# Gate projections cut by depth instead of by token half, in a hybrid attention and Mamba-2 layer

## The chip, the cores and the metric

The kernel runs on one core of a Trainium2 chip, as one launch. The metric is the device time in microseconds (us) of the whole launch. The engines named below are TensorE (PE, matmuls into PSUM), ScalarE (ACT), VectorE (DVE), GpSimd (POOL, here only a DMA queue) and SyncE (SP, a DMA queue). They run their own instruction streams in order and meet only at semaphores.

## The reference

One trunk layer over 128 context and 512 latent tokens, width 1024. What matters here is the mixer: one input projection gives attention heads, the scan's inputs, `z` and the gates, and the gates are used much later.

```python
def mixer(h, p, rope, ctx_k, ctx_v, h0_f, h0_b):
    proj = h @ p['w_in']
    q, k, v, z, xbc, dt, gates = jnp.split(proj, SPLIT_IDX, axis=-1)
    ...
    y_f, h_f = ssd_chunked(xs, dt_f, a[0], bm, cm, h0_f)
    y_b, h_b = ssd_chunked(flip(xs), flip(dt_b), a[1], flip(bm), flip(cm), h0_b)
    ...
    y = rms_norm(y * jax.nn.silu(z), p['ssd_norm'])
    g_a, g_b = jnp.split(gates, 2, axis=-1)
    merged = jax.nn.sigmoid(g_a) * (attn @ p['w_attn_o']) + jax.nn.sigmoid(g_b) * (y @ p['w_ssd_o'])
    return merged @ p['w_out'], k, v, h_f, h_b
```

## The kernel before

**Arithmetic.** Every large product is made of three matmuls of rounded parts, upper by upper (`whi`, `hh`), upper by lower (`whi`, `hl`) and lower by upper (`wlo`, `hh`). A block of weights is 1024 by 256. It comes by DMA into `raw` (`block` in the SP stream, L390), ACT rounds it into `whi` (`split_hi`, L1284) and DVE writes the rest into `wlo` (`split_lo`, L1749). There are two slots. Slot s is rounded anew only when PE has used it up, so `split_hi` of a block stands in ACT's stream right behind the read of the last result of the block two before.

**The scan with filling.** From about 523 to 906 us the kernel runs the Mamba-2 scan, chunk by chunk. Its steps are short and hang on each other across PE, ACT and DVE, so PE gets large independent matmuls between them, called pieces, written out by hand in a fixed order. `fill(n)` issues the next n pieces on PE, `weights(n)` does what belongs to the same pieces on ACT and on DVE, `weights(n)` in the SP stream issues weight loads (through `block_done`), and `stores(n)` on POOL writes results out. The first 40 pieces are tiles of `z`. The other 32 (n = 0 to 31) are the gate projections: 16 units of 128 gate channels, each over all 644 token columns, which lie in two halves of 322 columns (`HALF`) in two PSUM banks, `acc[:, 0]` and `acc[:, 1]`. Before the change a piece is one half: piece 2u fills bank 0 over the whole depth of 1024 (8 steps `k`, 24 matmuls), piece 2u + 1 fills bank 1. A piece waits until the piece two before it, which used the same bank, has been read out (`value(free, 2)`). ACT reads each piece out as soon as it comes to it (`out_of_acc`, L1296, 322 columns), and POOL stores a unit after its second piece.

**Where the pieces stand.** The scan has four latent chunks c = 1 to 4. Each runs `fill(F_LAT[c - 1])`, that is 3 pieces in a row, then `products`, then eight groups g = 0 to 7 with `fill(F_LAT_G[g])` and `scan_group(g, b, c)`; `F_LAT_G` is 1, 0, 1, 0, 1, 1, 0, 1. With the z tiles counted off, the gate pieces stand so:

- chunk 1: n = 0, 1, 2, 3 at groups 2, 4, 5, 7
- chunk 2: n = 4, 5, 6 at the start, then 7, 8, 9, 10, 11 at groups 0, 2, 4, 5, 7
- chunk 3: n = 12, 13, 14, then 15 to 19 likewise; chunk 4: n = 20, 21, 22, then 23 to 27
- behind the scan (`F_END` = 4): n = 28 to 31, and then attention

**What ACT has between the pieces at a chunk's start.** `exps(n)` (L1510, L1515) makes the decay weights of a group, and `squares(c, q)` (L1526) sums the squares of a gated quarter of y, which DVE has to have written (`gated`, L2050):

```python
            for c in range(1, NT):
                weights(1)
                exps(NG * c)
                if c > 1:
                    squares(c - 1, 2, zq[:, 0])
                weights(1)
                exps(NG * c + 1)
                if c > 1:
                    squares(c - 1, 3, zq[:, 1])
                weights(F_LAT[c - 1] - 2)
```

In front of the last quarters DVE has, in the group 7 of the chunk before: the lower part of a weight block (`split_lo`), `carried` (L2017 to L2031), `combined` (L2037) and `gated`.

**The z loads.** `z_in(c, q)` in the SP stream (L526) fetches a quarter of z for `gated(c, q)`; it stands behind group `Z_STEPS[q]` and waits for an earlier `squares`. In group 7 the SP stream also has a weight block (L390, 1 MB), which waits for a `split_lo`, and `h_in(c + 1, 1)` (L466, 512 KB).

The functions that the change touches, with the line numbers of the profile:

Of the kernel before, what the change touches and what calls it, by code (L numbers as in the profile page):

```python
# [8 lines left out]
ACT = mybir.ActivationFunctionType  # L9
# [4 lines left out]
P = 128  # L14
D = 1024
KT = D // P
# [22 lines left out]
HALF = TP // 2  # L39
NCONV = CTX + 2 + LAT  # L40
BW = 256
# [20 lines left out]
def value(c, back=0):  # L62

    v = c["step"] * (c["base"] + c["k"] - back)
    assert v > 0, "a wait stands where there is something to wait for"
    return v if c["round"] is None else c["round"] * (c["per"] * c["step"]) + v


def step(c, n=1):

    c["k"] += n
    return c["step"]


def due(c, back=0):

    step(c)
    return value(c, back)
# [27 lines left out]
def build(nc, a, outs):  # L106
# [16 lines left out]
    with ExitStack() as ctx:  # L123
# [207 lines left out]
        U_QKV = U_XBC + 2 * XBC // BW  # L331
        U_Z = U_QKV + 6 * NT
        U_G = U_Z + DI // BW * NT
        U_AO = U_G + 4 * 2 * D // BW
        U_SO = U_AO + KT
        U_OUT = U_SO + KT
        U_H2 = U_OUT + 4 * NT
# [18 lines left out]

        Y_ORDER = (1, 2, 3, 4, 0)
        Y_OUT = (1, 1, 2, 2, 3)
        Z_STEPS = (1, 2, 4, 6)
        GATED = {8 + 2 * q: q for q in range(4)}  # L360

        def block_done(p):
# [310 lines left out]
        def _(po):  # L673
# [65 lines left out]
            def stores(n):  # L739
                for p in range(pieces["k"], pieces["k"] + n):  # L740
                    if p < N_ZP:
                        step(free)
                        b, t = p // NT, p % NT
                        if t in (2, NT - 1):
                            part, z = (slice(0, 3), zo[0]) if t == 2 else (slice(3, NT), zo[1])
                            po.wait_ge(free["sem"], value(free))
                            po.dma_start(z_d.rearrange("t p c -> p t c")[:, part, b * BW:(b + 1) * BW],
                                         zst[:, part]).then_inc(z["sem"], step(z))
                    elif (p - N_ZP) % 2 == 1:
                        u = (p - N_ZP) // 2  # L750
                        step(free, 2)
                        po.wait_ge(free["sem"], value(free))
                        po.dma_start(g_d[u], gst[:, u % 2]).then_inc(go[u % 2]["sem"], step(go[u % 2]))
                step(pieces, n)

# [43 lines left out]
        def _(pe):  # L799
# [5 lines left out]
            def mul(out, l, r, first=True, last=True):  # L805
                return pe.matmul(out, l, r, start=first, stop=last)  # L806
# [203 lines left out]
                                   k == 0 and w is whi and m is hh, k == KT - 1 and m is hl)  # L1010
                last.then_inc(ready["sem"], step(ready))

            def gate_piece(n):

                unit, half = n // 2, n % 2
                slot, sub = unit // 2 % 2, unit % 2
                if n % 4 == 0:
                    pe.wait_ge(lo["sem"], due(lo))
                step(free)
                pe.wait_ge(free["sem"], value(free, 2))  # L1020
                for k in range(KT):
                    for w, m in ((whi, hh), (whi, hl), (wlo, hh)):
                        last = mul(acc[:, half, 0:HALF], w[:, slot, k, sub * P:(sub + 1) * P],
                                   m[:, k, half * HALF:(half + 1) * HALF],
                                   k == 0 and w is whi and m is hh, k == KT - 1 and w is wlo)
                last.then_inc(ready["sem"], step(ready))

            def fill(n):
                for p in range(pieces["k"], pieces["k"] + n):
                    if p < N_ZP:  # L1030
                        z_tile(p)
                    else:
                        gate_piece(p - N_ZP)
                step(pieces, n)

            btin, ctin, bnin = count(s["bt_in"], 16), pair("ct_in"), pair("bn_in")
# [238 lines left out]
        def _(act):  # L1275
# [17 lines left out]
            def out_of_acc(dst, src, func):  # L1293

                act.wait_ge(ready["sem"], due(ready))
                act.activation(dst, src, func).then_inc(free["sem"], step(free))  # L1296
# [175 lines left out]
            def weights(n):  # L1472

                for p in range(pieces["k"], pieces["k"] + n):
                    b = block_done(p)
                    if p < N_ZP:
                        z = zo[p % NT // 3]
                        if p % NT in (0, 3):
                            step(z)
                            act.wait_ge(z["sem"], value(z, 1))  # L1480
                        act.wait_ge(ready["sem"], due(ready))
                        act.activation(zst[:, p % NT], acc[:, p % 2, 0:BW], ACT.Tanh, scale=0.5).then_inc(s["zt_ok"], 1)
                    else:
                        u, half = (p - N_ZP) // 2, p % 2
                        if half == 0:
                            if u == 0:
                                for z in zo:
                                    act.wait_ge(z["sem"], value(z))
                            step(go[u % 2])
                            act.wait_ge(go[u % 2]["sem"], value(go[u % 2], 1))  # L1490
                        out_of_acc(gst[:, u % 2, half * HALF:(half + 1) * HALF], acc[:, half, 0:HALF], ACT.Copy)
                    if b is not None:
                        split_hi(b % 2)
                step(pieces, n)
# [866 lines left out]
```

## Time and profile before

| | |
|---|---|
| time before, median of 3 runs | 1839.19 us (1834.86 to 1839.99) |
| the profiled execution's own time | 1839.19 us |
| its span, first to last instruction | 1837.5 us |
| PE busy with matmuls | 1632.3 us (89% of the span) |
| DVE busy | 1031.7 us (56%) |
| ACT busy | 663.7 us (36%) |
| mean granted TensorE clock | 0.937 of full speed |

Times inside the profile count from the span's start. An engine's row in the timeline has its start, its duration, the line and the operation, what it writes and reads, how many instructions are merged, and in brackets how long the engine sat idle before it and who released it. Matmuls overlap: one of 322 columns is shown as 0.31 us, and the next starts 0.15 us behind it. A matmul is preceded by a weight load (LDWEIGHTS, the PEld rows). A row of a window has its bounds and length, then the busy time in it of PE, PEld, DVE, ACT and POOL with the number of instructions, then the granted clock of TensorE as a share of full speed (2.4 GHz; the other level is 1.2), the DMA engines' busy share and GB/s.

### The profile page before, as it was taken

How to read it: one execution, taken by the hardware profiler on the slowest of the kernel's cores; microseconds unless marked ns; L12 is line 12 of the kernel's file. 1: busy time of each engine (PE TensorE's matmuls, PEld its weight loads, DVE VectorE, ACT ScalarE, POOL GpSimd, SP SyncE). 2: the span in 40 equal slices, each digit the busy share in tenths (PEclk: the TensorE clock that was granted, in tenths of full speed). 3: DMA queues.
4: the chain of work that ended last, by engine and by line, in shares of the span. 5: the costliest groups of instructions: out<-in, count | busy, mean ns of one | idle time of the engine just before them, and what ended most of it. 6: DMA issues, size and time to landing. Idle time of an engine off the chain costs nothing.

```text
span 1837.5 us, 27440 instructions
## 1 busy us (share of the span) xinstructions
PE 1632.3 (89%) x11141; PEld 1538.5 (84%) x11141; DVE 1031.7 (56%) x1419; ACT 663.7 (36%) x1115; POOL 99.3 (5%) x155
## 2 busy tenths in 40 slices
PE   4799999989998998989799899989299999999995
PEld 2699988889998988888655699989199999999995
DVE  5466666556845578887555353335843343342467
ACT  4544443334365246667355432311321121111210
POOL 1000012110011100000000001000000000000000
PEclk9799999899999999999899999999599999999998
DMA  9344345532486676676600255342011222223221
GB/s 309 99 134 136 124 142 187 174 116 75 138 264 206 221 241 213 200 240 189 236 23 23 71 184 179 112 174 70 23 44 56 84 68 68 68 68 91 69 68 57
DMA packets 159721, 241.14 MB, mean 131 GB/s; under 512 B 8048, under 2 KB 126560, under 8 KB 156576
## 3 DMA queue, kind: packets, MB, share of 16 engines
q1 hardware_dynamic: 136464, 171.45, 28.8%
q0 software_dynamic: 12304, 47.72, 7.0%
q10 hardware_dynamic: 10880, 20.97, 4.2%
q8 instruction: 49, 0.80, 0.2%
q14 instruction: 24, 0.20, 0.0%
HBM read 195.06 MB, written 45.06 MB: 131 GB/s over the span
## 4 chain that ended last, share of the span: by engine, by line
PE 74%; DVE 14%; ACT 7%; issue 2%; DMA 1%; SPq 0%; ACTq 0%; DVEq 0%
PE acc L806 66%; PE tp L806 6%; DVE arena L1849 2%; ACT arena L1510 1%; DVE wlo L1749 1%; PE tp L1188 1%; DVE arena L2002 1%; ACT whi L1284 1%; DMA arena<-in_w_mod 1%; DVE arena L1788 1%; DVE arena L1787 1%; PE tp L889 1%; DVE wlo L1800 1%; DVE arena L2004 1%; DMA y_nat<-arena 1%
## 5 line engine op out<-in xcount | busy, mean ns | idle before, releaser
L806 PE MATMUL acc<-hh,whi 128*128 128x322 f32 x1408 | 363.4, 325 | 16.6 <-DVE wlo L1749 7.2
L806 PE MATMUL acc<-hl,whi 128*128 128x322 f32 x1408 | 357.4, 321 | 0.0
L806 PE MATMUL acc<-hh,wlo 128*128 128x322 f32 x1408 | 354.9, 319 | 0.0
L806 PEld LDWEIGHTS acc<-hh,whi 128*128 128x128 f32 x1408 | 254.1, 198 | 18.7 <-issue 12.2
L806 PEld LDWEIGHTS acc<-hl,whi 128*128 128x128 f32 x1408 | 255.2, 198 | 0.0
L806 PEld LDWEIGHTS acc<-hh,wlo 128*128 128x128 f32 x1408 | 254.1, 197 | 0.0
L1284 ACT ACTIVATE whi<-raw 128x2048 fp32r<-128x2048 f32 x78 | 148.7, 1908 | 266.2 <-PE acc L806 266.2
L1749 DVE TENSOR_TENSOR wlo<-raw,whi 128x2048 fp32r<-128x2048 f32 x78 | 178.5, 2290 | 101.5 <-ACT whi L1284 101.2
L806 PE MATMUL acc<-whi,hh 128*128 128x256 f32 x720 | 206.9, 287 | 8.0 <-DVE hl L2237 8.0
L806 PE MATMUL acc<-whi,hl 128*128 128x256 f32 x720 | 203.6, 283 | 0.0
L806 PE MATMUL acc<-wlo,hh 128*128 128x256 f32 x720 | 203.6, 283 | 0.0
L806 PE MATMUL acc<-whi,fh 128*128 128x256 f32 x640 | 183.2, 286 | 15.2 <-DVE fl L2299 15.2
L806 PE MATMUL acc<-wlo,fh 128*128 128x256 f32 x640 | 183.3, 286 | 0.0
L806 PE MATMUL acc<-whi,fl 128*128 128x256 f32 x640 | 182.8, 286 | 0.0
L806 PEld LDWEIGHTS acc<-whi,hh 128*128 128x128 f32 x720 | 137.4, 191 | 8.8 <-issue 8.4
L806 PEld LDWEIGHTS acc<-whi,fh 128*128 128x128 f32 x640 | 124.5, 195 | 16.3 <-issue 16.3
L806 PEld LDWEIGHTS acc<-wlo,hh 128*128 128x128 f32 x720 | 137.0, 190 | 0.3
L806 PEld LDWEIGHTS acc<-whi,hl 128*128 128x128 f32 x720 | 137.0, 190 | 0.0
L806 PE MATMUL tp<-arena 128*128 128x64 f32 (+3 forms) x508 | 115.6, 373 | 15.0 <-DVE arena L2004 10.0
L806 PEld LDWEIGHTS acc<-wlo,fh 128*128 128x128 f32 x640 | 124.3, 194 | 0.0
L806 PEld LDWEIGHTS acc<-whi,fl 128*128 128x128 f32 x640 | 124.2, 194 | 0.0
L1849 DVE SCALAR_TENSOR_TENSOR arena<-arena,colp 128x642 f32<-128x642 f32 x128 | 113.7, 888 | 18.7 <-DVE arena L1847 1.2
(255 smaller groups left out, 2327.0 us busy)
## 6 DMA issues: line engine op xcount, KB each, us to landing
raw<-in_w_in SPq DMA_DIRECT2D x38, 1024.0 KB, 7.0
raw<-in_w_mlp SPq DMA_DIRECT2D x32, 1024.0 KB, 5.4
arena<-in_w_mod SPq DMA_DIRECT2D x24, 1024.0 KB, 6.3
arena<-decay_sums_t ACTq DMA_DIRECT2D x40, 512.0 KB, 5.5
arena<-xs_nat SPq DMA_DIRECT2D x8, 1024.0 KB, 8.0
raw<-in_w_ssd_o SPq DMA_DIRECT2D x8, 1024.0 KB, 6.0
y_nat<-arena POOLq DMA_DIRECT2D x6, 1024.0 KB, 7.2
arena<-y_nat SPq DMA_DIRECT2D x6, 1024.0 KB, 6.4
```

The lines of the kernel that those rows point to most:

```text
L806: return pe.matmul(out, l, r, start=first, stop=last)
L889: last = pe.transpose(dst, cvs[:, n % 2, tok(t):tok(t) + P], ident)
L1188: last = pe.transpose(tp[:, j // 4, (j % 4) * P:(j % 4 + 1) * P], pr[:, u, j * P:(j + 1) * P], ident)
L1284: act.activation(whi[:, slot], raw[:, slot], ACT.Copy).then_inc(hi["sem"], step(hi))
L1510: last = act.activation(ee[:, b, d, r], abc[:, b, d, r], ACT.Relu, bias=dta[:, c, h:h + 1], scale=-1.0)
L1749: dve.tensor_tensor(wlo[:, slot], raw[:, slot], whi[:, slot].bitcast(F32), ALU.subtract).then_inc(lo["sem"], step(lo))
L1787: do(dve.scalar_tensor_tensor(x, x, mv[:, t, 0:1], rows[:, 0], ALU.subtract, ALU.mult))
L1788: return dve.scalar_tensor_tensor(x, x, mv[:, t, 2:3], rows[:, 1], ALU.mult, ALU.add)
L1800: dve.tensor_tensor(dst, src, upper.bitcast(F32), ALU.subtract).then_inc(mlo["sem"], step(mlo))
L1849: ins = dve.scalar_tensor_tensor(o, x[:, t:t + NCONV], w(t), o, ALU.mult, ALU.add)
L2002: last = dve.tensor_tensor(ee[:, b, d], ee[:, b, d], cbm[:, d, g].unsqueeze(1).broadcast_to([P, R, P]), ALU.mult)
L2004: dve.tensor_tensor(ee[:, b, 0], ee[:, b, 0], ee[:, b, 1], ALU.add).then_inc(m_ok["sem"], step(m_ok))
```

## The change

Three things change.

- A gate piece becomes half of the depth instead of half of the tokens (`gate_half`). Piece 2u runs k = 0 to 3 into both banks, piece 2u + 1 runs k = 4 to 7 into both banks. The matmuls of the two halves of the tokens with the same weights now stand next to each other. The number of matmuls in a piece stays 24, and their shape is the same.
- A unit is finished only with its second piece. Only then is it signalled, ACT reads both banks with one instruction of 644 columns, and `acc_ready` and `acc_free` count units and not pieces (`U_AO`). The first piece of a unit waits until the unit before has been read (`value(free, 1)`).
- `Z_STEPS` goes from (1, 2, 4, 6) to (1, 2, 5, 7).

```diff
@@ -331,7 +331,7 @@
         U_QKV = U_XBC + 2 * XBC // BW
         U_Z = U_QKV + 6 * NT
         U_G = U_Z + DI // BW * NT
-        U_AO = U_G + 4 * 2 * D // BW
+        U_AO = U_G + 2 * 2 * D // BW
         U_SO = U_AO + KT
         U_OUT = U_SO + KT
         U_H2 = U_OUT + 4 * NT
@@ -356,7 +356,7 @@
 
         Y_ORDER = (1, 2, 3, 4, 0)
         Y_OUT = (1, 1, 2, 2, 3)
-        Z_STEPS = (1, 2, 4, 6)
+        Z_STEPS = (1, 2, 5, 7)
         GATED = {8 + 2 * q: q for q in range(4)}
 
         def block_done(p):
@@ -748,8 +748,7 @@
                                          zst[:, part]).then_inc(z["sem"], step(z))
                     elif (p - N_ZP) % 2 == 1:
                         u = (p - N_ZP) // 2
-                        step(free, 2)
-                        po.wait_ge(free["sem"], value(free))
+                        po.wait_ge(free["sem"], due(free))
                         po.dma_start(g_d[u], gst[:, u % 2]).then_inc(go[u % 2]["sem"], step(go[u % 2]))
                 step(pieces, n)
 
@@ -1010,27 +1009,30 @@
                                    k == 0 and w is whi and m is hh, k == KT - 1 and m is hl)
                 last.then_inc(ready["sem"], step(ready))
 
-            def gate_piece(n):
-
-                unit, half = n // 2, n % 2
+            def gate_half(n):
+
+                unit, part = n // 2, n % 2
                 slot, sub = unit // 2 % 2, unit % 2
                 if n % 4 == 0:
                     pe.wait_ge(lo["sem"], due(lo))
-                step(free)
-                pe.wait_ge(free["sem"], value(free, 2))
-                for k in range(KT):
+                if part == 0:
+                    step(free)
+                    pe.wait_ge(free["sem"], value(free, 1))
+                for k in range(4 * part, 4 * part + 4):
                     for w, m in ((whi, hh), (whi, hl), (wlo, hh)):
-                        last = mul(acc[:, half, 0:HALF], w[:, slot, k, sub * P:(sub + 1) * P],
-                                   m[:, k, half * HALF:(half + 1) * HALF],
-                                   k == 0 and w is whi and m is hh, k == KT - 1 and w is wlo)
-                last.then_inc(ready["sem"], step(ready))
+                        for half in range(2):
+                            last = mul(acc[:, half, 0:HALF], w[:, slot, k, sub * P:(sub + 1) * P],
+                                       m[:, k, half * HALF:(half + 1) * HALF],
+                                       k == 0 and w is whi and m is hh, k == KT - 1 and w is wlo)
+                if part == 1:
+                    last.then_inc(ready["sem"], step(ready))
 
             def fill(n):
                 for p in range(pieces["k"], pieces["k"] + n):
                     if p < N_ZP:
                         z_tile(p)
                     else:
-                        gate_piece(p - N_ZP)
+                        gate_half(p - N_ZP)
                 step(pieces, n)
 
             btin, ctin, bnin = count(s["bt_in"], 16), pair("ct_in"), pair("bn_in")
@@ -1480,15 +1482,14 @@
                             act.wait_ge(z["sem"], value(z, 1))
                         act.wait_ge(ready["sem"], due(ready))
                         act.activation(zst[:, p % NT], acc[:, p % 2, 0:BW], ACT.Tanh, scale=0.5).then_inc(s["zt_ok"], 1)
-                    else:
-                        u, half = (p - N_ZP) // 2, p % 2
-                        if half == 0:
-                            if u == 0:
-                                for z in zo:
-                                    act.wait_ge(z["sem"], value(z))
-                            step(go[u % 2])
-                            act.wait_ge(go[u % 2]["sem"], value(go[u % 2], 1))
-                        out_of_acc(gst[:, u % 2, half * HALF:(half + 1) * HALF], acc[:, half, 0:HALF], ACT.Copy)
+                    elif (p - N_ZP) % 2 == 1:
+                        u = (p - N_ZP) // 2
+                        if u == 0:
+                            for z in zo:
+                                act.wait_ge(z["sem"], value(z))
+                        step(go[u % 2])
+                        act.wait_ge(go[u % 2]["sem"], value(go[u % 2], 1))
+                        out_of_acc(gst[:, u % 2].rearrange("p (a b) -> p a b", a=2), acc[:, 0:2, 0:HALF], ACT.Copy)
                     if b is not None:
                         split_hi(b % 2)
                 step(pieces, n)
```

## Rows read from the trace of the kernel before

**Rows 1.** Windows over chunks 3 and 4.

```profile
769.39:827.24 57.85, 51.44 (x322) 49.25 (x322) 48.19 (x68) 37.57 (x91) 2.69 (x5) 0.94 0.72 232
827.24:885.57 58.33, 50.71 (x306) 49.05 (x306) 42.38 (x58) 37.45 (x91) 2.69 (x5) 0.88 0.52 158
```

**Rows 2.** The chain that ended last, chunk 3: start us, us, what.

```profile
769.58 10.79 PE acc L806 x72
...
782.16 3.58 PE acc L806 x24
785.76 0.44 ACT arena L1296
...
788.03 2.29 DVE wlo L1749
...
792.31 7.39 PE acc L806 x32
```

**Rows 3.** Timeline of PE, chunk 2: the first matmul of piece 6.

```profile
718.93 0.31 PE L806 MATMUL acc<-hh,whi 128*128 128x322 f32 x1
```

**Rows 4.** Timeline of ACT, start of chunk 2.

```profile
721.72 0.63 ACT L1526 ACTIVATE cst<-arena 128x512 f32<-128x512 f32 x1 [1.73 <-DVE arena L2050]
...
722.35 0.42 ACT L1296 ACTIVATE arena<-acc 128x322 f32<-128x322 f32 x1
```

**Rows 5.** Groups by form on ACT: the two sizes of read-out of L1296.

```profile
L1296 ACT ACTIVATE arena<-acc 128x644 f32<-128x644 f32 x32 | 22.7, 710 | 99.4 <-PE acc L806 99.4
...
L1296 ACT ACTIVATE arena<-acc 128x322 f32<-128x322 f32 x32 | 13.6, 430 | 44.6 <-PE acc L806 44.6
```

**Rows 6.** Chain, PE's waits (total us, times, longest), PE's timeline, a window.

```profile
879.39 5.55 PE acc L806 x24
...
896.81 8.90 PE acc L806 x48
...
PE acc L806 <- ACT arena L1296: 4.4, 2, 3.8
...
734.64 0.69 PE L806 MATMUL acc<-arena 128*128 128x64 f32 x2 [3.16 <-DVE arena L2004]
...
731.40:742.00 10.60, 7.44 (x35) 7.34 (x35) 10.39 (x16) 7.25 (x19) 0.00 (x0) 0.68 1.00 358
```

**Rows 7.** Timelines of PE (chunks 3 and 4) and of ACT (chunk 4).

```profile
821.86 1.10 PE L806 MATMUL tp<-arena 128*128 128x64 f32 x8 [1.79 <-DVE arena L2004]
...
867.64 0.40 PE L806 MATMUL acc<-hh,whi 128*128 128x322 f32 x1
...
877.42 1.97 PE L806 MATMUL tp<-arena 128*128 128x64 f32 x8 [3.32 <-DVE arena L2004]
...
868.46 0.42 ACT L1296 ACTIVATE arena<-acc 128x322 f32<-128x322 f32 x1
```

**Rows 8.** Timeline of PE, a later stage that already pairs its matmuls.

```profile
1046.77 0.46 PE L806 MATMUL acc<-hl,whi 128*128 128x322 f32 x2
1047.07 0.46 PE L806 MATMUL acc<-hh,wlo 128*128 128x322 f32 x2
```

**Rows 9.** DVE at the start of chunk 3 and behind chunk 4.

```profile
780.00 0.69 DVE L2050 TENSOR_TENSOR arena<-arena,cst 128x512 f32<-128x512 f32 x1
...
782.20 1.23 DVE L1994 TENSOR_TENSOR arena<-tp,cst 128x1024 f32<-128x1024 f32 x1 [0.90 <-PE tp L806]
...
894.98 0.69 DVE L2050 TENSOR_TENSOR arena<-arena,cst 128x512 f32<-128x512 f32 x1
```

**Rows 10.** SP issues; then DMA issues with size and median us to landing.

```profile
773.92 0.46 SPq L466 DMA_DIRECT2D arena<-h_back  x1
...
889.55 0.38 SPq L390 DMA_DIRECT2D raw<-in_w_attn_o  x1
...
arena<-h_back SPq DMA_DIRECT2D x1, 512.0 KB, 6.2
...
cst<-z_nat SPq DMA_DIRECT2D x2, 256.0 KB, 11.3
```

## The prediction

> **What bounds the kernel now.** I read the page first, then the windows by chunk, then the chain that ended last inside the scan, and last the timelines of PE, ACT and DVE around every piece that the change touches.
>
> The page has PE busy 89% of the span. That says little about the changed stretch, because the matmuls of this stretch are the filling of a chain of short steps. The windows show it: a chunk lasts 57.85 us, and the next 58.33 us, with DVE busy 48.19 and 42.38 us of them [rows 1]. No engine is full, so the order of the waits decides.
>
> The chain of chunk 3 shows which waits those are [rows 2]. It begins on PE: three pieces in a row (10.79 us for 72 matmuls), `products`, and piece 15 (3.58 us). Then ACT reads piece 15 out (0.44 us), rounds a weight block (until 788.03), DVE writes its lower part (2.29, to 790.32) and weights group 1. Only then PE goes on at 792.31. The reader is to see two things. The first 16 us of each chunk run on PE alone, so whatever delays PE there delays the chunk. And nothing runs beside the chain that could take a delay in: piece 15 is what ACT and DVE wait for.
>
> **Part 1, the order of the matmuls.** The count stays 24 per piece, 768 in all, each with its own weight load. Before, neighbours have different weights, and 72 take 10.79 us, which is 150 ns each and 3.60 us for a piece [rows 2]. A later stage that already has neighbours with the same weights takes 0.30 us for two, from 1046.77 to 1047.07 [rows 8], the same 150 ns. I cost this part at 0.
>
> The Trainium skill, "TensorE: Matmul & The Clock Gate", section "Step-by-step: what each phase is for", says that weights typically stay put over many matmuls, so that one load can serve several. The trace does not show that here, since the paired stage runs at the same pace; what the rule would give stands with the rivals.
>
> **Part 2, the wait of a unit's first piece.** It is now behind the read-out of the whole unit before. There are 15 such places. ACT's place in its stream matters more than the length of its read-out.
>
> *Pieces 6, 14 and 22*, the third of three in a row. Before the change, piece 6 needed only piece 4's read-out, which ACT did in front of `exps`. Now it needs that of pieces 4 and 5, and this stands in ACT's stream behind `exps` and behind `squares(c - 1, 2)`, which waits for DVE. The rows give the moment: the `squares` start at 721.72, when DVE has let them go, and the read-out of piece 5 follows at 722.35 [rows 4]. Piece 6 began at 718.93 [rows 3]. After the change:
>
> - the read-out at 722.35 comes 0.28 us later, because what DVE waited for began with the read-out of piece 3, now 710 ns and not 430 [rows 5]: 722.63
> - it takes 0.71 us itself [rows 5]: 723.34, and some 0.05 us to PE: 723.4
>
> So piece 6 starts 4.45 us late. Chunks 3 and 4 repeat this pattern at the same offsets, so it is 3 x 4.45 = 13.4 us. By [rows 2] all of it is on the chain. What was queued behind piece 6 on PE is `products`, piece 7, and with it the weight block, group 1 and the rest. DVE's own wait in front of `products` (0.90 us [rows 9]) only grows.
>
> *The clock behind these waits.* PE sits idle some 4.3 us there. Before, it already goes idle once in each chunk, ahead of group 1: 3.16 us in chunk 2, and the window around that has a granted clock of 0.68 [rows 6], so most of it ran at 1.2 and not at 2.4 GHz. What this costs is read from the chain: behind the same idling in chunk 3, 8 scan matmuls and a piece take 7.39 us [rows 2], where full clock gives 1.10 [rows 7] + 3.60 = 4.70 us, so 2.7 us; behind 877.42 it is 1.97 + 5.55 - 4.70 = 2.8 us [rows 6, 7]; behind the 3.8 us of idling ahead of 896.81, 48 matmuls take 8.90 us and not 7.2, so 1.7 us [rows 6]. The bounds are 0 and 2.8. I take 2.3: 3 x 2.3 = 6.9 us.
>
> *Pieces 2, 10, 18 and 26* at group 5. They now wait for the unit that ended at group 4, which ACT reads behind an `exps`. In chunk 4 this read-out starts at 868.46 and would end at 869.17, where piece 26 began at 867.64 [rows 7]: 1.6 us late. But PE idles 3.32 us soon after, ahead of 877.42 [rows 7], so this costs nothing, and it cuts that idling into about 1.4 and 1.7 us. Idling of that length (1.79 us ahead of 821.86) left the clock up: the 8 matmuls behind it took 1.10 us, not 1.97 [rows 7]. I therefore expect the slow stretch behind 877.42 to go: -2.8 us. The bound on the other side is 0. In the other three chunks the wait is 0.5 us, in front of an idling of 1.3 us; nothing.
>
> *Pieces 4, 8, 12, 16, 20, 24 and 28* stand behind a scan group or behind a read-out that is long done: 0.1 us at most. *Piece 30* is in part 4.
>
> **Part 3, one read-out of 644 columns.** It is 0.28 us longer than one of 322 [rows 5]. On the chain it stands behind pieces 7, 15 and 23, ahead of the rounding of a block: 3 x 0.28 = 0.8 us. That of pieces 3, 11 and 19 is in part 2 already. ACT loses 16 of 32 read-outs, about 16 x 0.43 x 2 - 16 x 0.71 = 2.4 us of work, none of it on the chain.
>
> **Part 4, the z loads and the end.** Moving the third from behind group 4 to behind group 5 changes nothing, since the SP stream has nothing between. The fourth is moved past the weight block and past `h_in`, and these wait for a `split_lo` of group 7. It is issued at about 774.4 instead of before 764. `h_in`, issued at 773.92 behind the block, landed after 6.2 us, at 780.1 [rows 10], so this quarter of z should land at about 781. `gated` wanted it at 780.00, and DVE then waited until 782.20 for `products` [rows 9], which now come 4 us later still. So 0, three times; without that cover it would be 1 us each.
>
> Behind chunk 4 there is no cover. The load is issued right behind the block of 889.55 [rows 10], so at about 890.2 with the longer read-out before it, and lands near 896, where `gated` started at 894.98 [rows 9]: 0.8 us. The worst landing of such loads in the trace is 11.3 us [rows 10], which would make it 6. The chain to piece 30 also has the longer read-outs of pieces 27 and 29, and behind 31 a third: 0.8 us. For a somewhat longer slow clock behind piece 30 I add 0.5. Together 2.1 us.
>
> **The sum.** 13.4 + 6.9 - 2.8 + 0.8 + 2.1 = 20.4 us on the profiled execution's 1839.19 us, which is also the median: 1859.6 us, rounded to 1860. Behind the scan nothing changes, and attention starts from piece 31's read-out, so the delay should arrive whole.
>
> **The rivals.**
>
> *A. Only the read-out itself is waited for* (no measurable change). The wait of pieces 6, 14, 22 and 30 would be the 0.71 us of the read-out and a signal, so 0.75 x 4 = 3 us, and no slow clock. With the read-outs on the chain (0.8 + 0.8) and no saved slow stretch: 1844 us; with it 1841. It needs ACT to be free when piece 5 ends. For it: ACT has an idle stretch of 1.73 us there. Against it: that idling ends with `squares`, which stand ahead of the read-out [rows 4].
> The Trainium skill, "Perfetto Trace Analysis", section "Matmuls", has the rule behind it, that independent groups should rotate through PSUM banks so that the read-out of one runs beside the next. It speaks against this change, and by it alone the price is one read-out per unit in a row; the trace agrees that before, with two banks in turn, piece 6 had no wait.
>
> *B. Matmuls with the same weights run faster* (faster than before). The weight loads fill PE's load side as much as the matmuls do (49.25 us of loads beside 51.44 us of matmuls in chunk 3 [rows 1]), so if the loads set the 150 ns and half of them became free, a matmul would go down. 28 of the 32 pieces lie on the chain (not those at group 5), 672 matmuls. It outweighs the 20.4 us from 30 ns each, and shows as faster from (20.4 + 5.5) / 672 = 39 ns; at a pace of 110 ns the time would be 1859.6 - 26.9 = 1833 us. Against it stands the equal pace of the stage that pairs them [rows 8].
> The sentence of the Trainium skill on loading once, cited above, would lead here; by it the change is a gain, and the paired stage does not bear it out.
>
> *C. The z loads are late as well* (slower still). If the fourth quarter lands 11.3 us after its issue [rows 10], that is at 785.7, DVE is still done before `products` come at about 786.8, so only the end pays: 5 us more, 1865; with a clock price of 2.8 and no saved stretch behind 877.42, 1869 us.
>
> **How the numbers follow.** The forecast, three waits of more than 4 us with a slow clock behind them, has 0.78; C has 0.08, A 0.08, B 0.06. What a measurement of this kernel can tell from no change is 0.3%, 5.5 us. The forecast's own range: with clock prices of 0 to 2.8 us, the saved stretch there or not, and the end at 1.6 to 7 us, it runs from 1839.2 + 13.4 + 0 - 2.8 + 0.8 + 1.6 = 1852 to 1839.2 + 13.4 + 8.4 + 0.8 + 7 = 1869. To 1850 and 1868 leaves out A and B and a little of C, under 2 in 10. A is half below 1845, so slower by over 0.3% is 0.87, within it 0.08, faster 0.05.
>
> **What would show it.** In the profile after, PE should sit idle about 4.3 us ahead of the third piece of chunks 2, 3 and 4, put down to ACT L1296, and the piece behind it should take about 5.5 us and not 3.6. The three chunk windows should grow by about 7 us each, chunk 4's by less, with granted clocks under 0.94. L1296 should have 16 read-outs fewer of 322 and 16 more of 644 columns at 710 ns. The matmuls inside a piece should keep 150 ns. It would be wrong if ACT reads pieces 4 and 5 before `squares`, if the idle stretch is there but the clock stays up, or if DVE's `gated` waits for a DMA ahead of `products`.

## The result and the profile after

| | before | after |
|---|---|---|
| median | 1838.51 us (1834.86 to 1839.99, 4 runs) | 1858.80 us (1855.09 to 1859.84, 4 runs) |
| the profiled execution: time, span | 1839.19, 1837.5 us | 1860.62, 1858.9 us |
| mean granted clock | 0.937 | 0.936 |

The ratio is 1.011, 95% interval [1.0089, 1.0131]: slower by 1.1%, and 1.2 us from the forecast of 1860. The read-out is L1298 now, the matmul L805, `squares` L1527, `gated` L2051.

First the windows, from one chunk start to the next (chunks 2, 3, 4):

```profile
709.67:773.91 64.24, 53.59 (x321) 50.89 (x321) 48.20 (x68) 37.23 (x87) 2.72 (x5) 0.92 0.66 209
773.91:840.05 66.14, 55.45 (x321) 52.75 (x321) 48.20 (x68) 37.22 (x87) 2.70 (x5) 0.90 0.64 203
840.05:903.50 63.45, 51.82 (x304) 49.65 (x305) 42.47 (x58) 37.11 (x87) 2.70 (x5) 0.87 0.45 146
```

Chunks 3 and 4 took 57.85 and 58.33 us [rows 1], chunk 2 took 57.69 (its pieces 4 and 12 start at 711.70 and 769.39). The three sum to 193.83 us instead of 173.87, so 20.0 us come in here. DVE is busy as long as before (48.20 us in chunk 3, before 48.19), ACT a little less (37.2 and 37.6). PE's clock is lower, 0.92, 0.90 and 0.87 against 0.94 and 0.88 in [rows 1].

The chain that ended last shows what the length is. The rows start at the beginning of chunk 3, with the `gated` of the third quarter of the y of chunk 2 (start us, us, what; in all chains "..." stands for rows left out):

```profile
783.23 0.70 DVE arena L2051
...
784.49 0.19 ACT cst L1527
784.67 0.60 ACT arena L1298
...
785.32 5.35 PE acc L805 x24
790.67 1.78 PE tp L805 x16
792.46 3.61 PE acc L805 x24
```

In chunk 3 before, the chain began on PE and stayed there for 16 us [rows 2]. Now it comes out of DVE: `gated`, then ACT's `squares` (the row at 784.49 is their end), then the read-out of pieces 12 and 13, and only then the third piece, 14. PE's timeline puts the idle time at that same point, and ACT's timeline in chunk 2 shows the order on its side:

```profile
785.32 0.68 PE L805 MATMUL acc<-hh,whi 128*128 128x322 f32 x2 [4.06 <-ACT arena L1298]
```

```profile
719.72 0.63 ACT L1527 ACTIVATE cst<-arena 128x512 f32<-128x512 f32 x1 [4.37 <-DVE arena L2051]
...
720.35 0.69 ACT L1298 ACTIVATE arena<-acc 128x644 f32<-128x644 f32 x1
```

ACT sits idle for 4.37 us in front of `squares`. The read-out that PE waits for stands behind them in ACT's stream, and its second piece was done at 717.07. The three idle stretches of PE are 4.02, 4.06 and 4.06 us. The third pieces behind them take 5.21, 5.35 and 6.44 us, where the piece in the chain above, at 792.46, takes 3.61. In the groups by form the read-outs of 322 columns are gone:

```profile
L1298 ACT ACTIVATE arena<-acc 128x644 f32<-128x644 f32 x48 | 33.9, 706 | 145.3 <-PE acc L805 145.3
```

That is 16 more than the 32 of [rows 5]. The end of the scan, on the same chain:

```profile
896.30 1.10 PE tp L805 x8
897.41 5.16 PE acc L805 x24
...
905.20 2.30 DVE wlo L1750
...
907.52 0.38 SPq L390
...
907.95 6.36 DMA cst<-z_nat
...
914.40 0.70 DVE arena L2051
...
915.85 0.60 ACT arena L1298
...
916.50 9.94 PE acc L805 x48
```

The last quarter of z is on the chain: it is asked for only when the lower part of the weight block is written and the next block issued (907.52). From piece 28 to the end of piece 31 it is 22.9 us (903.50 to 926.4), where it was 20.1 (885.57 to 905.7). The first four matmuls of attention then take 2.93 us instead of 1.56. DVE's waits for z, in total, times, longest:

```profile
DVE arena L2051 <- DMA cst<-z_nat: 13.5, 4, 4.6
```

Before there was no such wait. Three of the four are off the chain. DVE's timeline in chunk 3 shows why:

```profile
789.15 0.69 DVE L2051 TENSOR_TENSOR arena<-arena,cst 128x512 f32<-128x512 f32 x1 [4.63 <-DMA cst<-z_nat]
...
792.50 1.23 DVE L1995 TENSOR_TENSOR arena<-tp,cst 128x1024 f32<-128x1024 f32 x1 [2.05 <-PE tp L805]
```

DVE loses 4.63 us to the fourth quarter of z, and then still has to wait 2.05 us for `products`, which are late themselves.

From the start of piece 28 to the end of the span, before took 951.9 us and after 955.4: +3.5. With the +20.0 this is 23.5 us; the two spans differ by 21.4, because chunk 2 began 2.0 us earlier in this execution (709.67 against 711.70). That start scatters from run to run: in the kernels below that add nothing to PE's program it lies between 702.31 and 713.33.

### The profile page after: what moved, and what is told of

Read it like the earlier page. It is cut to its first block, busy times and chain, and to the rows that moved or that the text cites. A ratio compares the mean times of both kernels' runs of the same rounds, so it can differ in the third digit from the quotient of the medians.

```text
span 1858.9 us, 27421 instructions
## 1 busy us (share of the span) xinstructions
PE 1638.2 (88%) x11141; PEld 1542.0 (83%) x11141; DVE 1031.8 (56%) x1419; ACT 662.4 (36%) x1099; POOL 99.5 (5%) x155
## 4 chain that ended last, share of the span: by engine, by line
PE 72%; DVE 15%; ACT 7%; issue 3%; DMA 2%; SPq 0%; ACTq 0%; DVEq 0%
PE acc L805 64%; PE tp L805 5%; DVE arena L1850 2%; DVE wlo L1750 2%; ACT arena L1511 1%; ACT whi L1286 1%; PE tp L1190 1%; DVE arena L2003 1%; DMA arena<-in_w_mod 1%; PE tp L888 1%; DVE arena L1789 1%; DVE arena L1788 1%; ACT arena L1298 1%; DVE wlo L1801 1%; DVE arena L2005 1%
## 5 line engine op out<-in xcount | busy, mean ns | idle before, releaser
L805 PE MATMUL acc<-hh,whi 128*128 128x322 f32 x1408 | 343.3, 326 | 33.3 <-ACT arena L1298 20.1
L805 PE MATMUL acc<-hl,whi 128*128 128x322 f32 x1408 | 336.5, 321 | 0.0
L805 PE MATMUL acc<-hh,wlo 128*128 128x322 f32 x1408 | 333.2, 319 | 0.0
L805 PEld LDWEIGHTS acc<-hh,whi 128*128 128x128 f32 x1408 | 248.0, 199 | 37.1 <-ACT arena L1298 21.7
L805 PEld LDWEIGHTS acc<-hl,whi 128*128 128x128 f32 x1408 | 250.5, 198 | 0.0
L805 PEld LDWEIGHTS acc<-hh,wlo 128*128 128x128 f32 x1408 | 248.8, 197 | 0.0
L805 PE MATMUL acc<-whi,hh 128*128 128x256 f32 x720 | 207.6, 288 | 7.9 <-DVE hl L2238 7.9
L805 PE MATMUL acc<-whi,hl 128*128 128x256 f32 x720 | 204.3, 284 | 0.0
L805 PE MATMUL acc<-wlo,hh 128*128 128x256 f32 x720 | 204.1, 283 | 0.0
L805 PE MATMUL acc<-whi,fh 128*128 128x256 f32 x640 | 182.7, 285 | 15.2 <-DVE fl L2300 15.2
L805 PE MATMUL acc<-wlo,fh 128*128 128x256 f32 x640 | 182.7, 286 | 0.0
L805 PE MATMUL acc<-whi,fl 128*128 128x256 f32 x640 | 182.4, 285 | 0.0
L805 PEld LDWEIGHTS acc<-whi,hh 128*128 128x128 f32 x720 | 138.1, 192 | 8.8 <-issue 8.4
L805 PEld LDWEIGHTS acc<-wlo,hh 128*128 128x128 f32 x720 | 137.7, 191 | 0.3
L805 PEld LDWEIGHTS acc<-whi,hl 128*128 128x128 f32 x720 | 137.6, 191 | 0.0
L805 PEld LDWEIGHTS acc<-whi,fh 128*128 128x128 f32 x640 | 124.0, 194 | 16.3 <-issue 16.3
L805 PE MATMUL tp<-arena 128*128 128x64 f32 (+3 forms) x508 | 113.9, 370 | 11.9 <-DVE arena L2005 8.4
L805 PEld LDWEIGHTS acc<-wlo,fh 128*128 128x128 f32 x640 | 123.8, 193 | 0.0
L805 PEld LDWEIGHTS acc<-whi,fl 128*128 128x128 f32 x640 | 123.6, 193 | 0.0
```

## The experiments

"Sum of the chunks" below is always the three windows of chunks 2, 3 and 4: 173.87 us before, 193.83 us in the profile after. "Behind piece 28" is from its start to the end of the span: 951.9 us before, 955.4 after. "Waits" are PE's idle times ahead of pieces 6, 14 and 22, and these are the "third pieces". All of these are of one profiled execution; the ratio is that of the times to the kernel before, measured beside it on the same chip.

### The changed kernel again

The changed kernel as it is, measured once more.

> The changed kernel as it is, beside the others of this call, for a ratio with as many runs as theirs. 1.0110 of the kernel before, as first measured, within 0.2%.

1.0129 [1.0108, 1.0151]; waits 4.05, 4.06, 4.02; third pieces 6.50, 5.23, 5.35; sum of the chunks 190.56, behind piece 28 955.0. The sum is 3.3 us less than in the first profile of the same kernel. Two slow stretches, 8 scan matmuls and piece 19 or 27, ran at full clock this time (pieces 19 and 27 take 3.84 us, and took 5.06 and 5.34). The timelines of PE ahead of piece 19, first of the profile after, then of this run:

```profile
832.81 1.47 PE L805 MATMUL tp<-arena 128*128 128x64 f32 x8 [1.79 <-DVE arena L2005]
```

```profile
835.96 1.10 PE L805 MATMUL tp<-arena 128*128 128x64 f32 x8 [1.78 <-DVE arena L2005]
```

The same idle time before, at one and the same place, once with the clock low and once not.

### The waits without the pairs

```diff
-                for k in range(4 * part, 4 * part + 4):
+                half = part
+                for k in range(KT):
                     for w, m in ((whi, hh), (whi, hl), (wlo, hh)):
-                        for half in range(2):
...
```

The order of the matmuls of before, with all waits, read-outs and z loads of the changed kernel.

> The changed kernel with its waits, its one read-out of 644 columns per unit and its Z_STEPS, but the matmuls in the old order: the first piece of a unit fills one bank over the whole depth, the second the other, so no neighbours share weights. My theory (the order of the matmuls costs and gives nothing): the same time as the changed kernel, 1857 to 1861. Rival B in the weak form that pairing gives some ns per matmul back: 1863 to 1870.

1.0126 [1.0111, 1.0141], against 1.011 and 1.0129 with pairs. Waits 4.03, 4.03, 4.01; third pieces 6.47, 5.18, 5.38; sum of the chunks 190.57, where the changed kernel has 190.56. The pairs are worth nothing. Rival B falls.

### Read out before the squares

```diff
                 weights(1)
                 exps(NG * c)
+                weights(1)
                 if c > 1:
                     squares(c - 1, 2, zq[:, 0])
-                weights(1)
                 exps(NG * c + 1)
```

> The changed kernel with one move in ACT's stream: at the start of chunks 2 to 4 the read-out of the first unit stands ahead of squares(c - 1, 2) and not behind it. My theory: PE's wait ahead of pieces 6, 14 and 22 falls from 4.0 us to about 0.7 (the read-out of 0.71 us and a signal) and the clock stays up there, so 3 x (3.3 + 1.6 to 2.8) = 15 to 18 us come back: 1841 to 1845. If not the place in ACT's stream but something else of the changed structure costs the time: 1855 to 1859.

1.0028 [1.0014, 1.0042], so 0.01 lower than the changed kernel as measured again, some 18 us (15 against its first ratio). ACT's timeline in chunk 2, then PE's:

```profile
720.83 0.71 ACT L1298 ACTIVATE arena<-acc 128x644 f32<-128x644 f32 x1 [1.81 <-PE acc L805]
723.38 0.64 ACT L1527 ACTIVATE cst<-arena 128x512 f32<-128x512 f32 x1 [1.84 <-DVE arena L2051]
```

```profile
721.59 0.56 PE L805 MATMUL acc<-hh,whi 128*128 128x322 f32 x2 [0.86 <-ACT arena L1298]
```

ACT now waits for PE, reads at once, and PE stands still for 0.86 us and not 4.05. The third pieces take 3.83 us, so the low clock behind them is gone too. The sum of the chunks is 178.07. This is rival A's time (one read-out and a signal), made by moving one line. What made the wait dear was ACT's order and not the read-out.

### The z loads alone, and all but them

In the one kernel only `Z_STEPS` of before becomes (1, 2, 5, 7); in the other only `Z_STEPS` of the changed kernel goes back to (1, 2, 4, 6).

> The kernel before with the new Z_STEPS alone. My theory (the time comes from three waits of PE for ACT's read-out, which stands behind squares, and from the slow clock behind them): the late fourth quarter of z costs little. At the chunk boundaries DVE waits about 1 to 2 us for it, but products come 4 us sooner here than in the changed kernel, so up to 1 us per boundary may reach the chain; at the end of the scan 1 to 3 us. Time 1840 to 1844. Rival C (the z loads are what costs): 1850 or more. No effect at all: 1838.5.

> The changed kernel with the old Z_STEPS. My theory: PE's waits of 4.0 us ahead of the third piece of chunks 2, 3 and 4 stay; the end of the scan gets back about 2 us of the 5.6 us of idling ahead of piece 30. Time 1855 to 1858 against 1858.8. Rival C: under 1850.

Alone: 1.0018 [1.0007, 1.003]. Taken back: 1.0096 [1.0076, 1.0117]. DVE's waits, then PE's timeline ahead of piece 30, both of the kernel with the z loads alone:

```profile
DVE arena L2050 <- DMA cst<-z_nat: 4.9, 4, 1.3
```

```profile
899.27 0.64 PE L806 MATMUL acc<-hh,whi 128*128 128x322 f32 x1 [5.12 <-ACT arena L1296]
```

The sum of the chunks is 173.56, as before, although three of the waits lie there: they are covered. Behind piece 28 it is 955.2, +3.3: 1.3 us more idle (5.12 against 3.84), the 48 matmuls behind it 10.06 us and not 8.90, and attention's first four 2.93 and not 1.56, all three seen in the trace; 0.5 us of it is made up later. With the z steps taken back, the changed kernel's idle time is 4.14 us and `gated` waits for no DMA; behind piece 28 it is 952.5, so 2.5 us less than the changed kernel. The two ratios, 1.0129 and 1.0096, differ by 6 us, but their intervals leave room for anything from next to nothing to twice that.

### Both repairs

The changed kernel with `weights(1)` ahead of the squares and the old z steps.

> The changed kernel with both repairs: the first unit of chunks 2 to 4 is read out ahead of squares, and the old Z_STEPS. What is left of the change is the paired order, one read-out per unit and waits of under 1.5 us. My theory: within 0.2% of the kernel before (ratio 0.999 to 1.002), since read_before_squares gave 1.0028 and the z loads alone 1.0018. A rival by which the pairs pay would show as under 0.998.

1.0029 [1.0012, 1.0046]: a miss. Waits 0.86 three times, behind piece 28 952.7, but the sum of the chunks 180.39, 6.5 us above before, where three waits of 0.86 explain 2.6. In chunks 2 and 3 the piece at group 7 is slow (766.70 to 771.98 and 828.34 to 833.55, so 5.3 and 5.2 us, where it takes 3.8 in before). Much of what was left looked like clock, so the next kernels keep PE from falling idle.

### Matmuls in the wait

24 matmuls of 190 columns into unused PSUM columns, behind the second piece of three in a row (n = 5, 13, 21). Their result is used nowhere.

```diff
+                if n in (5, 13, 21):
+                    last = keep_busy(24)
                 if part == 1:
                     last.then_inc(ready["sem"], step(ready))
```

> The changed kernel with 24 extra matmuls of 190 columns, whose results nobody reads, behind pieces 5, 13 and 21; they fill part of the idle 4.0 us and carry the signal that the unit is done. They split the price of a wait from the price of the clock behind it. My theory: the third pieces still start when they did, but take 3.6 to 3.8 us and not 5.2 to 6.4, so 3 x 1.6 to 2.8 = 5 to 8 us come back: ratio to the kernel before 1.0065 to 1.0085. If the slow clock is not set off by this idling: no change, 1.011. If the extra matmuls last longer than the wait: slower.

1.0133 [1.011, 1.0156], no gain: a miss. Yet in the chunks it did what it was to do: idle 1.40, 1.35, 1.41 us, third pieces 3.83, 3.82, 3.84. The sum is 186.86 and not 190.56, so 3.7 us come back and not 5 to 8; pieces 19 and 27 were slow again here (5.23 and 5.35 us). Behind piece 28 it took 962.0 us, 7 more than the changed kernel, in stages that the edit does not touch. PE's waits behind 1300 us (in total, times, longest) have a row that the changed kernel doesn't have there:

```profile
PE acc L805 <- issue: 3.3, 2, 1.7
```

"issue" is idle time in which PE waited for nothing that the profile shows. These waits are 3.3 of the 7 us; the rest is not placed.

### The kernel before, kept busy at group 1

20 such matmuls ahead of group 1 of each latent chunk, behind a wait for the read-out of the piece before.

> The kernel before with 20 extra matmuls of 190 columns, whose results nobody reads, in the idling ahead of group 1 of chunks 1 to 4 (3.2 to 4.0 us), where the clock falls. If the slow clock follows from the idling: each of the four stretches behind it (7.0 to 7.45 us) falls to about 4.7, so 9 to 11 us less, ratio 0.994 to 0.995. If the extra matmuls outlast DVE's work: the gain is smaller or gone. If the clock falls for another reason: 1.000.

1.0023 [1.0006, 1.0039]: a miss, for two reasons. The stretches behind group 1 do run at full clock (4.73 us in chunk 4 and not 7.45), but three times 2.5 to 2.7 us give only 3.9 in the chunks (58.05, 57.57, 54.33). Piece 11 was slow in this execution (5.12 us, before 3.81), which takes 1.3 of the rest. The chain that ended last shows more, in chunk 2 and then in chunk 3:

```profile
728.52 1.21 DVE arena L2010 x2
...
730.37 0.68 DVE arena L1997
731.05 0.60 DVE arena L2025
731.65 0.61 DVE arena L2027
```

```profile
779.05 12.32 DMA arena<-decay_sums_t
...
793.88 9.22 DMA arena<-decay_sums_t
```

From 728.52 to 758.66 it runs on DVE with hardly a gap. In chunk 3 it runs over two loads of the decay sums that `exps` needs; the chain of the kernel before has none there. So with PE faster, DVE in one chunk and these loads in another are the next bound. And behind piece 28 it is 956.9 us, +5.0, again with "issue" waits (3.2 us in 2).

### Only a longer program

288 waits on a count long reached, ahead of the first turning of x. They come to 144 more wait instructions on PE (the trace has 144 instructions more). No work is added.

```diff
+            for _ in range(288):
+                pe.wait_ge(s["rows_in"], 16 * 9)
             turn_x(xin, "xn_ok", NT)
```

> The kernel before with 144 wait instructions more in TensorE's program (288 waits in the source, two to an instruction), ahead of the first turning of x, each on a count that is long reached; no other work is added or moved. Two kernels with dummy matmuls (24 behind pieces 5, 13 and 21 of the changed kernel; 20 ahead of group 1 in the kernel before) both took some 5 us longer in the MLP stage, which holds none of the dummies, with TensorE's idle put down to 'issue' there (3.2 to 3.3 us). Theory (A): the length of TensorE's program ahead of the MLP's loop sets where its instructions lie, and the fetch of them stalls; then this kernel is some 5 us above before, ratio 1.0020 to 1.0035, with the same 'issue' waits in the MLP stage. Rival (B): the dummies cost the MLP their time through the clock or through order of the work, not through the program's length; then this kernel is within 1.5 us of before (ratio 0.999 to 1.001), and shows no such 'issue' waits.

1.008 [1.0061, 1.0099], more than expected. PE's timeline where they stand, then PE's waits behind 1300 us:

```profile
68.46 1.94 PE L847 MATMUL acc<-cst,arena 128*128 128x128 f32 x8 [11.73 <-issue]
```

```profile
PE acc L806 <- issue: 5.5, 3, 1.9
```

PE stands for 11.7 us at the 144 instructions, some 81 ns each, which I had left out; chunk 2 starts only 6.2 us later (717.88), so a part is made up on the way. Behind piece 28 it is 960.3 us, +8.4, of which 5.5 are the "issue" waits; behind two of the three the clock is low as well. So rival B falls, and of theory A this much holds: a longer program of PE, with no matmul added, brings the waits in the MLP. That it is the fetch of instructions is not shown. Nor is length alone the rule: the last three kernels have 126 added matmuls, some 256 instructions with their weight loads, and none of them shows an "issue" wait there. So these three can be compared with the kernels that have no such wait.

### The changed kernel kept busy, 126 matmuls

24 behind n = 5, 13, 21 and 29, and 15 ahead of group 1 of chunks 2 and 3.

> The changed kernel with 24 dummy matmuls of 190 columns behind pieces 5, 13, 21 and 29, and 15 ahead of group 1 in chunks 2 and 3, so that TensorE doesn't stand idle through the 4 us waits; 126 matmuls, some 256 instructions more in all. Theory (A), the clock's fall costs what its stretches show (third pieces 6.4, 5.2, 5.3 against 3.83, sum about 5.5 us; some of it given back by the vector engines): chunk periods sum to 183 to 187 us against 190.6 of the changed kernel, and the time lies 3 to 7 us below it, ratio to before 1.009 to 1.011, if the MLP stage is as long as in the changed kernel; with the MLP's 5 us on top, ratio 1.012 to 1.014. Rival (B), what the low clock costs is only exchanged for waits for VectorE: the sum stays within 2 us of 190.6, ratio 1.012 to 1.014 with no MLP stall.

1.0069 [1.005, 1.0088]. PE's timeline in chunk 2, and the three windows:

```profile
720.55 2.82 PE L805 MATMUL acc<-hh 128*128 128x190 f32 x24
724.72 0.57 PE L805 MATMUL acc<-hh,whi 128*128 128x322 f32 x2 [1.36 <-ACT arena L1308]
```

```profile
713.31:774.98 61.67, 55.16 (x360) 52.66 (x360) 48.10 (x68) 37.23 (x87) 2.71 (x5) 0.97 0.66 218
774.98:836.60 61.62, 55.14 (x360) 52.64 (x360) 48.11 (x68) 37.24 (x87) 2.69 (x5) 0.97 0.66 218
836.60:897.10 60.50, 51.53 (x328) 49.45 (x329) 42.46 (x58) 37.22 (x87) 2.69 (x5) 0.94 0.46 152
```

The waits are as long as before (2.82 + 1.36 us), but filled. The clock is 0.97, 0.97 and 0.94, the sum 183.79, 6.8 us under 190.56, inside theory A's 183 to 187; rival B falls. Behind piece 28 it is 951.6, 3.4 less than the changed kernel, as the 48 matmuls of pieces 30 and 31 now take 7.4 us and not 9.6. A had left this gain out, so the ratio came out below its range of 1.009 to 1.011.

### The kernel before, and the repaired one, kept busy with as many

22 matmuls behind piece 29 and 104 at groups 1 (in the kernel before 84 there and 20 at group 6 of chunk 4).

> The kernel before with 22 dummy matmuls of 190 columns behind piece 29, 21 ahead of group 1 of chunks 1 to 4, and 20 ahead of group 6 of chunk 4: 126 matmuls, some 256 instructions more. The dummies fill the idle after which the clock was seen to fall. Theory (A), VectorE is the chain once the stretches run at full clock: the latent stage is 0 to 3 us shorter, and with no stall in the MLP the time is 0.998 to 1.000 of before, with it 1.000 to 1.003. Rival (B), the low clock is paid in full: four stretches of 7.45 against 4.73 us and one of 5.2 against 3.6 give 10 us back, ratio 0.994 to 0.997. If TensorE's program length is what stalls the MLP, this kernel, 256 instructions longer, may have a stall of another size than the ones with 144 to 165 more.

> The changed kernel with both repairs (ScalarE's second read-out of a chunk ahead of the squares, and z rows asked for in steps 1, 2, 4, 6), and with 26 dummy matmuls of 190 columns ahead of group 1 of chunks 1 to 4 and 22 behind piece 29: 126 matmuls, as many as in the kernel before with dummies, which came to 0.9967 [0.9949, 0.9986]. Without dummies the two repairs left 1.0029 [1.0012, 1.0046], three waits of 0.86 us and chunk periods that sum to 180.4 us against 173.9. Theory (A), what the repairs leave is mostly TensorE at low clock in the stretches behind group 1 and group 6, and only 2.6 us of waits: the periods sum to 174 to 178 us and the ratio is 0.997 to 1.000. Rival (B), the read-out in pairs holds the chain up in itself (ScalarE and VectorE work in another order), whatever the clock: the periods stay above 179 us and the ratio at 1.001 to 1.004. Either way it doesn't beat the kernel before with dummies by more than the interval.

The kernel before so filled: 0.9967 [0.9949, 0.9986], medians 1832.29 against 1836.85 us; its runs lie 0.8% apart (1822.09 to 1836.9). It is 0.3% faster than the kernel before, and so than every form of the changed one without fillers. The repaired one: 0.9986 [0.9972, 0.9999]. The windows of the one, then of the other:

```profile
704.80:761.67 56.87, 51.62 (x344) 49.02 (x343) 48.10 (x68) 37.59 (x91) 2.72 (x5) 1.00 0.74 236
761.67:820.28 58.61, 53.12 (x343) 50.49 (x343) 48.21 (x68) 37.58 (x91) 2.70 (x5) 0.97 0.73 229
820.28:873.11 52.83, 50.01 (x347) 48.36 (x347) 42.12 (x58) 37.35 (x91) 2.70 (x5) 1.00 0.57 175
```

```profile
703.33:762.02 58.69, 53.77 (x346) 51.06 (x347) 48.11 (x68) 37.35 (x87) 2.71 (x5) 0.97 0.72 229
762.02:820.21 58.19, 52.54 (x346) 49.52 (x347) 48.02 (x68) 37.33 (x87) 2.69 (x5) 1.00 0.71 231
820.21:874.41 54.20, 48.92 (x330) 46.57 (x331) 42.20 (x58) 37.25 (x87) 2.69 (x5) 1.00 0.55 170
```

The sums are 168.31 and 171.08. The kernel before gets back 5.6 us in these chunks, more than the 0 to 3 of theory A and less than rival B's full price, which is 10.7 us here (three stretches behind group 1 and the one behind 877.42). Its ratio is in B's range. Piece 19 was slow in this execution (5.36 us), and the loads of the decay sums are on its chain too, the longest with 12.9 us. The repaired one gets back 9.3 us (180.39 to 171.08), more than theory A expected, and lies 2.8 us above the kernel before so filled, where three waits of 0.86 make 2.6. So what the waits leave of the change is small here. It is not zero for certain: each sum is of one execution, and both of these executions are among the fastest of their kernels (1824.8 and 1827.0 us, medians 1832.29 and 1831.64); the intervals of the two ratios overlap.

## Why the prediction was right

The time was right, and so were the main mechanism and most terms of the sum. One by one:

- **The order of the matmuls, 0.** Right. 48 matmuls from 709.67 to 717.07 keep the 150 ns, and the same kernel without the pairs has the same time. The Trainium skill, "TensorE: Matmul & The Clock Gate", section "Step-by-step: what each phase is for", says that one weight load can serve several matmuls; here each matmul of a pair still had its own, 321 loads beside 321 matmuls in the window of chunk 3.
- **Three waits, 13.4.** The mechanism was right. The idle stretches are 4.02, 4.06 and 4.06, 12.1 us. Piece 6 starts 11.41 us behind the chunk's first piece and not 7.23 [rows 3], so it is 4.18 us late and not 4.45. The missing 0.28 us, the longer read-out of piece 3, is not gone: it comes ahead of the chunk's first piece. Piece 4 waits for that read-out and starts 0.95 us behind the end of piece 3, where it was 0.65. Pieces 12, 20 and 28 do the same, so 3 x 0.3 = 0.9 us lie in the three chunks. The forecast had given these places 0.1 us at most.
- **The clock behind them, 6.9.** Third pieces of 5.21, 5.35 and 6.44 against 3.83 us at full clock make 5.5, so 1.8 each and not 2.3. The kernel with these waits filled and 126 matmuls added fits that size with 6.8 us less in the chunks, though it also fills two places at group 1 and so holds a little of theirs. With the read-out moved, waits and clock go together.
- **The saved slow stretch of chunk 4, -2.8.** Half shown. Piece 26 waited 1.36 us (1.4 forecast) and the idling was cut in two; then 1.10 + 5.16 us stood against 1.97 + 5.55 [rows 6, 7], so 1.3 saved. In the second profile this piece ran at full clock (898.81 to 902.65, so 3.84 us), and nearly all of the 2.8 was saved. Against that, the first profile had a new slow stretch in chunk 3, 1.47 + 4.83 us, that the forecast did not have: 1.6.
- **Longer read-outs, 0.8.** About right. From the start of piece 7 to that of piece 8, which holds one of them, it is 12.49 us and was 12.14; in chunks 3 and 4 it is 12.48 and was 12.13 and 12.15. Together that is 1.0 us.
- **The z loads, 0 three times and 2.1 at the end.** Right that the three of the chunks cost nothing, but not for the reason given. I had `gated` find this quarter landed; DVE waited 4.63 us for it ahead of `products`, which the forecast had named as a sign of being wrong. The load was issued at 778.97 and came in at about 789.1, so after some 10 us and not the 6.6 of the forecast. Only the lateness of `products` covered it, with 2.05 us to spare. At the end the term was too small: +3.5 us, and the kernel with the z loads alone has +3.3. The idle stretch ahead of piece 30 grew by 1.8 us (1.4 forecast, from z and two read-outs). The larger part is the clock: I gave the 48 matmuls 0.5 us more of it, and they took 1.0 more, and the first four matmuls of attention, which the forecast left alone, took 1.4 more. Some 1 us of this is made up before the end of the span.

By the trace the sum is 12.5 (three late starts) + 0.9 (pieces 12, 20 and 28) + 5.5 - 1.3 + 1.6 + 1.0 + 3.5 = 23.7 us; 23.5 were found between the marks. The forecast had 20.4. It came within 1.2 us of the median partly by luck: the clock behind the waits was put too high, the saved stretch too high as well, the end too low, and the start of chunk 2 scatters by more than that. Measured again, the changed kernel was 1.0129 of the kernel before, which is 23.7 us. Rival A fell by the 4 us waits, and would have been the outcome with ACT's stream in another order. B fell by the kernel without pairs. C was right that z was late in the chunks and that this costs nothing there; at the end, where it had 5 us more, z landed after 6.4 us and not 11.3.

## What to carry to other kernels

Before a wait is tied to a larger unit of work, look up where the instruction that releases it stands in its engine's stream: the read-out itself was 0.7 us, and what stood ahead of it made it 4. Price an idle stretch of TensorE with the low clock behind it, here about half as much again as the waits themselves. And an experiment that adds instructions needs a look at the stages that it does not touch, and a control with as many instructions: added ones moved a later stage by 5 us and more here.

## What the runs showed that was not expected

- A longer instruction stream on TensorE can cost time elsewhere: with 144 waits added ahead of `turn_x`, 5.5 us of "issue" idling in the MLP, 1.9 us the longest, and 3.3 and 3.2 us in the two kernels with 72 and 80 added matmuls. With 126 added matmuls (some 256 instructions) there was none, in three kernels. The cause stays open.
- A row of satisfied waits is not free: PE stood for 11.7 us at 144 of them, 81 ns each. Whether that is the wait itself or getting the instructions, the run does not separate.
- The granted clock doesn't follow from the length of the idling before: behind 1.79 us it fell in one execution (8 matmuls in 1.47 us, then a piece of 4.83) and behind 1.78 us it stayed up in another (1.10 us), at the same place of one kernel. A price for it can only be a mean of such cases; two profiles of the changed kernel differ by 3.3 us through them.
- Matmuls of 190 columns came every 110 ns (24 in 2.82 us, of which the last is shown with 0.28), those of 322 columns every 150: two fifths of the columns less save only a quarter of the time.
